# One place in each round for the score products, the value products and the transposes of two attentions, in a two-block network kernel

## The chip, the cores and the metric

The kernel runs on one core of one Trainium2 chip, in one launch. The metric is the device time of that launch in microseconds (us). TensorE (PE in the rows) does the matrix products and the transposes, and PEld is its weight load; ScalarE is ACT, VectorE is DVE, GpSimd is POOL, and SyncE (SP) issues most of the transfers.

## What is computed

A sequence of 512 tokens of width 1024 goes through two blocks of a network, all in fp32. The first block is a Mamba-2 mixer and then a layer of stick-breaking attention (16 heads of 64). The second is a gated linear recurrence beside a band attention (8 heads of 64), then a feed-forward network and a gated side input. The change touches the two attentions alone:

```python
# stick-breaking attention, for each block of 128 queries (lo..hi) and each head
z = jnp.einsum('bthd,bshd->bhts', q[:, lo:hi], k[:, :hi]) * scale
log_keep = jnp.where(mask, jax.nn.log_sigmoid(-z), 0.0)
after = lax.cumsum(log_keep, axis=3, reverse=True) - log_keep
a = jnp.exp(jnp.where(mask, jax.nn.log_sigmoid(z) + after, -jnp.inf))
outs.append(jnp.einsum('bhts,bshd->bthd', a, v[:, :hi]))
...
# band attention, second block
scores = jnp.einsum('bnqhd,bnkhd->bnhqk', qc, kb) * (B_HD ** -0.5)
probs = jax.nn.softmax(scores + bias, axis=-1)
o = jnp.einsum('bnhqk,bnkhd->bnqhd', probs, vb)
```

## The kernel before

Each large product of activations with a weight matrix is cut into output blocks of 128 features by 512 tokens. Both factors are split into a high and a low part, so each 128-row slice of the inner dimension takes three TensorE instructions, L658 (high by high), L659 and L660: a *step* of the text below. The activations' parts lie in HH and HL (SH and SL, WH and WL for some products), the weights' in whi and wlo. ScalarE makes whi from the loaded chunk (raw) with one instruction, L1985, and VectorE makes wlo (L1257).

Beside this dense stream run the attentions. Their work is cut into *units* a. A unit is a pair of heads and one block of 128 queries: 32 units in the stick-breaking attention, 16 in the band attention. The number of keys of a unit is 512, 384, 256, 128 for a mod 4 = 0, 1, 2, 3 in the first, and 128, 256, 384, 512 in the second, so that a tile of both heads has up to 1024 columns. A unit goes through these stages (the lines of the first attention first, of the band attention in brackets):

- TensorE: scores QK into PSUM tile zz, L985 (L1120), two products with 64 rows of weights
- first attention: ScalarE reads zz twice, sigmoid of -z and of z (L2319, L2320); VectorE scans (L1604) and multiplies (L1610). Band: VectorE reads zz with scale and bias (L1816), takes the maximum (L1818), ScalarE takes the exponential (L2475), VectorE divides (L1828, L1829)
- TensorE: transposes the weights into PSUM tile tt, L961 (L1095), 128x128 each
- ScalarE: copies tt to SBUF, L2325 (L2482)
- TensorE: values AV, L973 (L1108), products with 64 columns of weights, into bank 7; after each fourth unit ScalarE copies bank 7 out (L2330, L2490)

There is one zz and one tt. QK of unit a waits until zz is free of unit a-1 (semaphore s_bk, which L2320 raises; in the band s_bs, which L1816 raises), and the transposes of a wait until tt is free of a-1 (s_at; s_bt2).

Work of different units overlaps by *rounds* r. Each engine has a generator, `attention()` or `band()`, that yields three times in each round, and a generator with its share of the dense work. `weave` walks the two side by side in the ratio of their weights (111 to 120 in the first attention, 60 to 87 in the band), and so fixes the order of instructions on the engine: each engine runs strictly in that order. On TensorE the three places of round r hold the transposes of unit r-2, the values of r-3 and the scores of r+1. On ScalarE they hold the sigmoids of unit r, the copy of tt of unit r-2, and the copy of bank 7; between them `weave` puts what the dense work needs from ScalarE: the copy of a query block out of its bank (L2283), a tanh of a gate (L2302), SH from OZ (L2310) and the weights' whi (L1985).

Of the kernel before, what the change touches and what calls it, by code (L numbers as in the profile page):

```python
# [14 lines left out]
S = 512  # L15
# [183 lines left out]
def program(nc, wstream, astream, tstream, crow, vec, con, masks, xT, pT, rbx, out, scratch, pscr):  # L199
# [26 lines left out]
    zz, tt = (ctx.enter_context(nc.psum_tensor(n, [128, 2, S], F32)) for n in ("zz", "tt"))  # L226
# [33 lines left out]
    KT = sbt("KT", [128, NB, S], F32, ph)  # L260
    VT = sbt("VT", [128, 4, D], F32, ph)
    QT = sbt("QT", [128, NB, S], F32, ph)
# [18 lines left out]
    QB = sbt("QB", [128, 4, S], F32, phb)  # L281
    KB = sbt("KB", [128, 4, S], F32, phb)
# [20 lines left out]
    PS = [sbt(f"PS{i}", [128, 2, S], F32, ph3) for i in range(2)] + [TT3[:, 1:3, :]]  # L303
# [20 lines left out]
    ident, ones, bones = ccol("ident"), ccol("ones"), ccol("bones")  # L324
# [31 lines left out]
    s_kt, s_vt, s_qt, s_sz = (sem(n) for n in ("s_kt", "s_vt", "s_qt", "s_sz"))  # L356
    s_szt, s_qk, s_tr, s_av = (sem(n) for n in ("s_szt", "s_qk", "s_tr", "s_av"))
    s_bk, s_ls, s_at, s_o, s_go = (sem(n) for n in ("s_bk", "s_ls", "s_at", "s_o", "s_go"))
# [6 lines left out]
    s_off, s_ho, s_hoc, s_osq, s_osum, s_or, s_on, s_oah, s_oal = (  # L365
        sem(n) for n in ("s_off", "s_ho", "s_hoc", "s_osq", "s_osum", "s_or", "s_on", "s_oah", "s_oal"))
    s_qb, s_nsq, s_nsum, s_nr, s_qn, s_vb = (sem(n) for n in ("s_qb", "s_nsq", "s_nsum", "s_nr", "s_qn", "s_vb"))
    s_ga, s_wa, s_gb, s_wb, s_bw = (sem(n) for n in ("s_ga", "s_wa", "s_gb", "s_wb", "s_bw"))
    s_bq, s_bs, s_bm, s_be, s_bp, s_btr, s_bt2, s_bv, s_bo, s_obh, s_obl = (
        sem(n) for n in ("s_bq", "s_bs", "s_bm", "s_be", "s_bp", "s_btr", "s_bt2", "s_bv", "s_bo", "s_obh", "s_obl"))  # L370
# [74 lines left out]
    rows_of = lambda a: 3 - a % 4  # L445
    width = lambda a: 128 * (rows_of(a) + 1)
    att = lambda a, hi: W[:, 2 * (a % 4):2 * (a % 4) + 2, 0:hi]
    keeps = flat(W[:, 8:14, :])[:, 0:4 * (S + 1)].rearrange("p (a s) -> p a s", a=4)
    keep = lambda a, c0, c1: keeps[:, 2 * (a % 2):2 * (a % 2) + 2, c0:c1]
    live = lambda *units: [a for a in units if 0 <= a < 32]  # L450

    some = lambda a: [a] if 0 <= a < 16 else []
# [175 lines left out]
    def _(e):  # L628
        w = Once(e)
# [203 lines left out]
        for n, src in ((0, dd), (1, ac)):  # L833
            for c in range(4):
                o = 128 * n + 32 * c
                x = e.transpose(bank[:, o:o + 32], src[:, 128 * c:128 * c + 128], ident[0:32, 0:32])
# [4 lines left out]
                 start=True, stop=True).then_inc(s_sel, 1)  # L841
# [36 lines left out]
        for n in range(8):  # L878
            if n == 4:
                sum_of("out", aux[0])  # L880
            o, c = aux[1 + n % 4][:, :], slice(128 * n, 128 * n + 128)
# [3 lines left out]
            for k in range(2):  # L885
# [3 lines left out]
                x = e.matmul(o, wl[:, k, c], PH[:, k, :], start=False, stop=(k == 1))  # L889
# [61 lines left out]

        def attention():
            for r in range(-1, 36):
                for a in live(r - 2):
                    w.wait_ge(s_ls, a + 1)
                    w.wait_ge(s_at, a)
                    w.wait_ge(s_vt, 8)
                    for j in range(2):
                        for b in range(rows_of(a) + 1):
                            c = slice(128 * b, 128 * b + 128)  # L960
                            x = e.transpose(tt[:, j, c], att(a, S)[:, j, c], ident)  # L961
                    x.then_inc(s_tr, 1)
                yield
                for a in live(r - 3):
                    n, tb = a // 4, rows_of(a)
                    w.wait_ge(s_at, a + 1)
                    w.wait_ge(s_vt, 8)
                    if a % 4 == 0:
                        w.wait_ge(s_o, n)
                    for b in range(tb + 1):  # L970
                        for j in range(2):
                            h = 2 * n + j
                            x = e.matmul(aux[4][64 * j:64 * j + 64, 128 * tb:128 * tb + 128], VT[:, b, 64 * h:64 * h + 64],  # L973
                                         att(a, S)[:, j, 128 * b:128 * b + 128], start=(b == 0), stop=(b == tb))
                    x.then_inc(s_av, 1)
                yield
                for a in live(r + 1):
                    n, hi = a // 4, width(a)
                    w.wait_ge(s_qt, n + 1)
                    w.wait_ge(s_kt, n + 1)  # L980
                    w.wait_ge(s_vt, 6)
                    w.wait_ge(s_bk, a)
                    for j in range(2):
                        o = 64 * j
                        x = e.matmul(zz[:, j, 0:hi], QT[o:o + 64, n, hi - 128:hi], KT[o:o + 64, n, 0:hi],  # L985
                                     start=True, stop=True)
                    x.then_inc(s_qk, 1)
                yield

        proj = sb_proj()  # L990
# [1 line left out]
        next(proj)  # L992
        so_first = both("so", 0, "so")
        weave((attention(), 111), (chain(proj, take(so_first, 6)), 120))
        run(so_first)
        for n in range(2, 8):
# [12 lines left out]
        for t in range(4):  # L1009
            x = e.matmul(aux[4][:, t:t + 1], R[:, 128 * t:128 * t + 128], ident[:, 0:1], start=True, stop=True)  # L1010
# [75 lines left out]

        def band():
            for r in range(-1, 19):
                for a in some(r - 2):
                    w.wait_ge(s_bp, a + 1)  # L1090
                    w.wait_ge(s_bt2, a)
                    for j in range(2):
                        for b in range(a % 4 + 1):
                            c = slice(128 * b, 128 * b + 128)
                            x = e.transpose(tt[:, j, c], PS[a % 3][:, j, c], ident)  # L1095
                    x.then_inc(s_btr, 1)
                yield
                for a in some(r - 3):
                    n, tb = divmod(a, 4)
                    w.wait_ge(s_bt2, a + 1)  # L1100
                    w.wait_ge(s_vb, 4)
                    if tb == 0:
                        w.wait_ge(s_bo, n)
                        w.wait_ge(s_rc, 1)
                    for b in range(tb + 1):
                        for j in range(2):
                            h = 2 * n + j
                            x = e.matmul(aux[4][64 * j:64 * j + 64, 128 * tb:128 * tb + 128], VB[:, b, 64 * h:64 * h + 64],  # L1108
                                         PT[:, j, 128 * b:128 * b + 128], start=(b == 0), stop=(b == tb))
                    x.then_inc(s_bv, 1)  # L1110
                yield
                for a in some(r + 1):
                    n, tb = divmod(a, 4)
                    hi = 128 * (tb + 1)
                    w.wait_ge(s_qn, 8)
                    w.wait_ge(s_or, 4)
                    w.wait_ge(s_bs, a)
                    for j in range(2):
                        o = 64 * j
                        x = e.matmul(zz[:, j, 0:hi], QB[o:o + 64, n, 128 * tb:hi], KB[o:o + 64, n, 0:hi],  # L1120
                                     start=True, stop=True)
                    x.then_inc(s_bq, 1)
                yield

        def gates_a():
# [17 lines left out]
        dense_a = chain(gates_a(), branch_a())  # L1143
        run(take(dense_a, 5))
        weave((band(), 60), (dense_a, 87))
        for i2 in range(2):
            for n in range(4 * i2, 4 * i2 + 4):
# [1581 lines left out]
```

## Time and profile before

| | |
|---|---|
| time, median of 3 runs | 1557.64 us (1557.12 to 1559.62) |
| profiled execution, first to last instruction | 1557.7 us |
| TensorE busy | 1542.0 us, 99% |
| VectorE busy | 950.1 us, 61% |
| ScalarE busy | 678.2 us, 44% |
| mean granted clock of TensorE | 0.998 of full |
| first attention | about 523 to 669 us of the span |
| band attention | about 938 to 1035 us |

The profiled execution is one run of the same program. Its span agrees with the median of the runs to 0.1 us, and no other time of its own is listed. Starts in the trace's rows are in us from the start of the span. A matrix product's row gives its start and a modelled duration, and the durations of products in a row overlap, so that TensorE's pace is read from start to start.

### The profile page before, as it was taken

The page shows a single profiled execution, that of the slowest core. Times are in us where ns is not written, and L with a number is a line of the kernel's source. Part 1 is how long each engine was busy: PE and PEld are TensorE (multiplying, and loading weights), DVE is VectorE, ACT ScalarE, POOL GpSimd, SP SyncE. Part 2 cuts the span into 40 slices and gives each one's busy share as a digit, 9 for nine tenths or more (in the row PEclk, how much of TensorE's full clock was granted, in tenths as well). Part 3 has the DMA queues.
Part 4 walks back from the last instruction along what each step waited for, and adds up shares of the span by engine and source line. Part 5 has one row for each costly group of instructions (what it writes and reads, how often), then busy time and mean ns, then how long its engine had stood idle before and what let it go on. Part 6 is the DMA issues. An engine that isn't in the chain of part 4 may idle for free. (4 is left out here: it accounts for less than half of the span.)

```text
span 1557.7 us, 19286 instructions
## 1 busy us (share of the span) xinstructions
PE 1542.0 (99%) x7818; PEld 1220.9 (78%) x7818; DVE 950.1 (61%) x1211; ACT 678.2 (44%) x958; POOL 97.5 (6%) x66
## 2 busy tenths in 40 slices
PE   8999999999999999999999999999999999999998
PEld 4788887878788666678898886678888888888887
DVE  4769798996884666755468446754554434432445
ACT  4555676754432655654222455533342222322232
POOL 0000001011300000013000000000120000000110
PEclk9999999999999999999999999999999999999999
DMA  9245344433792111123211123222223222222233
GB/s 390 85 162 177 126 130 139 149 100 133 264 365 97 69 55 33 49 81 102 92 55 55 55 82 95 68 82 85 105 81 108 85 105 96 94 101 101 76 113 122
DMA packets 47383, 177.72 MB, mean 114 GB/s; under 512 B 3616, under 2 KB 20512, under 8 KB 31680
## 3 DMA queue, kind: packets, MB, share of 16 engines
q1 hardware_dynamic: 30368, 167.44, 30.2%
q10 hardware_dynamic: 16928, 9.06, 2.2%
q8 instruction: 62, 1.02, 0.3%
q14 instruction: 25, 0.20, 0.0%
HBM read 172.23 MB, written 4.26 MB: 113 GB/s over the span
## 5 line engine op out<-in xcount | busy, mean ns | idle before, releaser
L658 PE MATMUL bank<-HH,whi 128*128 128x512 f32 x1352 | 556.3, 411 | 0.5 <-issue 0.4
L660 PE MATMUL bank<-HH,wlo 128*128 128x512 f32 x1352 | 528.9, 391 | 0.0
L659 PE MATMUL bank<-HL,whi 128*128 128x512 f32 x1352 | 528.1, 391 | 0.0
L1257 DVE TENSOR_TENSOR wlo<-raw,whi 128x2048 fp32r<-128x2048 f32 (+2 forms) x122 | 267.2, 2190 | 105.7 <-ACT whi L1985 105.3
L658 PEld LDWEIGHTS bank<-HH,whi 128*128 128x128 f32 x1352 | 254.3, 188 | 81.0 <-issue 33.5
L660 PEld LDWEIGHTS bank<-HH,wlo 128*128 128x128 f32 x1352 | 254.2, 188 | 55.1
L659 PEld LDWEIGHTS bank<-HL,whi 128*128 128x128 f32 x1352 | 254.9, 189 | 47.9 <-issue 3.8
L1985 ACT ACTIVATE whi<-raw 128x2048 fp32r<-128x2048 f32 (+2 forms) x118 | 222.4, 1885 | 127.5 <-PE bank L660 108.2
L2587 POOL TENSOR_TENSOR SR<-SR,tmp 128x512 f32<-128x512 f32 x35 | 62.1, 1773 | 596.1 <-ACT tmp L2005 595.1
L1604 DVE TENSOR_TENSOR_SCAN W<-W,cc 128x511 f32<-128x511 f32 (+3 forms) x64 | 49.0, 808 | 34.6 <-ACT W L2320 34.5
L660 PE MATMUL bank<-FH,wlo 128*128 128x512 f32 x176 | 68.5, 389 | 0.0
L659 PE MATMUL bank<-FL,whi 128*128 128x512 f32 x176 | 68.5, 389 | 0.0
L658 PE MATMUL bank<-FH,whi 128*128 128x512 f32 x176 | 68.5, 389 | 0.0
L1916 DVE TENSOR_TENSOR pst<-bank,SR 128x512 f32<-128x512 f32 x22 | 15.1, 692 | 71.9 <-PE bank L660 71.9
L1928 DVE SCALAR_TENSOR_TENSOR tmp<-tmp,bank 128x512 f32<-128x512 f32 x22 | 15.1, 688 | 64.9 <-PE bank L660 64.9
L2556 ACT ACTIVATE FH<-tmp 128x512 fp32r<-128x512 f32 x22 | 13.9, 633 | 85.9 <-DVE tmp L1928 85.9
L2552 ACT ACTIVATE tmp<-pst 128x512 f32<-128x512 f32 x22 | 13.9, 633 | 82.4 <-DVE pst L1916 82.4
L2005 ACT ACTIVATE tmp<-X 128x512 f32<-128x512 f32 x35 | 21.6, 626 | 61.5 <-DVE X L1476 44.8
L2587 POOL TENSOR_TENSOR SR<-SR 128x512 f32<-128x512 f32 x12 | 19.9, 1662 | 340.7 <-ACT SR L2005 340.7
L2147 ACT ACTIVATE E<-AC,atk 128x128 f32<-128x128 f32 x128 | 39.1, 392 | 4.8 <-DMA AC<-scratch 4.8
L2319 ACT ACTIVATE W<-zz 128x1024 f32<-128x1024 f32 (+3 forms) x32 | 22.6, 708 | 41.1 <-PE zz L985 37.3
L658 PE MATMUL bank<-WH,whi 128*128 128x512 f32 x96 | 38.9, 405 | 0.0
(328 smaller groups left out, 2228.2 us busy)
## 6 DMA issues: line engine op xcount, KB each, us to landing
raw<-wstream SPq DMA_DIRECT2D x113, 1024.0 KB, 4.9
aslot<-tstream SPq DMA_DIRECT2D x24, 512.0 KB, 3.7
A<-astream SPq DMA_DIRECT2D x8, 1024.0 KB, 20.6
AC<-scratch ACTq DMA_DIRECT2D x16, 512.0 KB, 5.4
QT<-tstream SPq DMA_DIRECT2D x12, 512.0 KB, 6.5
OZ<-tstream SPq DMA_DIRECT2D x12, 512.0 KB, 7.7
raw<-wstream SPq DMA_DIRECT2D x4, 768.0 KB, 4.3
X<-xT SPq DMA_DIRECT2D x1, 2048.0 KB, 8.4
```

What stands on the lines that cost most here:

```text
L658: e.matmul(o, wh[:, k, c], hi[:, kb0 + k, :], start=first and k == 0, stop=False)
L659: e.matmul(o, wh[:, k, c], lo[:, kb0 + k, :], start=False, stop=False)
L660: x = e.matmul(o, wl[:, k, c], hi[:, kb0 + k, :], start=False, stop=last and k == kb - 1)
L1257: x = e.tensor_tensor(wlo[:, i % 2, c], raw[:, i % 2, c], whi[:, i % 2, c].bitcast(F32), ALU.subtract)
L1604: x = e.tensor_tensor_scan(k, k, diag[:, last], 0.0, ALU.mult, ALU.add)
L1916: e.tensor_tensor(pstage[n % 3][:, :], bank_of("fg", n)[:, :], R, ALU.mult).then_inc(s_fgr, 1)
L1928: e.scalar_tensor_tensor(q, q, 0.5, bank_of("fu", n)[:, :], ALU.mult, ALU.mult).then_inc(s_fu, 1)
L1985: e.activation(whi[:, i % 2, 0:n], raw[:, i % 2, 0:n], ACT.Copy).then_inc(s_hi, 1)
L2005: e.activation(dst, src, ACT.Square, scale=scale).then_inc(s_sq, 1)
L2147: x = e.activation(E[(u + 1) % 2][:, h, :], AC[:, h, :], ACT.Relu, scale=-1.0, bias=atk[:, cv_, 8 * gv + h:8 * gv + h + 1])
L2319: e.activation(keep(a, S - hi, S), zz[:, :, 0:hi], ACT.Sigmoid, scale=-1.0)
L2587: e.tensor_tensor(acc, acc, tile, ALU.add).then_inc(s_sqa, 1)
```

## The change

The three parts of a round on TensorE move to its third place, in the order scores of r+1, values of r-3, transposes of r-2. The first two places become empty. It is done in both attentions, and on no other engine does the order of instructions change.

```diff
         def attention():
             for r in range(-1, 36):
-                for a in live(r - 2):
-                    w.wait_ge(s_ls, a + 1)
-                    w.wait_ge(s_at, a)
-                    w.wait_ge(s_vt, 8)
+                yield
+                yield
+                for a in live(r + 1):
+                    n, hi = a // 4, width(a)
...
+                    w.wait_ge(s_bk, a)
                     for j in range(2):
...
+                        x = e.matmul(zz[:, j, 0:hi], QT[o:o + 64, n, hi - 128:hi], KT[o:o + 64, n, 0:hi],
+                                     start=True, stop=True)
+                    x.then_inc(s_qk, 1)
                 for a in live(r - 3):
                     n, tb = a // 4, rows_of(a)
                     w.wait_ge(s_at, a + 1)
...
                     x.then_inc(s_av, 1)
-                yield
-                for a in live(r + 1):
...
+                for a in live(r - 2):
+                    w.wait_ge(s_ls, a + 1)
+                    w.wait_ge(s_at, a)
+                    w.wait_ge(s_vt, 8)
                     for j in range(2):
...
+                            x = e.transpose(tt[:, j, c], att(a, S)[:, j, c], ident)
+                    x.then_inc(s_tr, 1)
                 yield
```

The change in `band()` is the same, with its own tiles and semaphores. In the changed file QK, AV and the transposes of the first attention stand at L964, L976 and L986, those of the band at L1099, L1112 and L1121.

TensorE in round 3 of the first attention, before: values of unit 0 (L973), scores of unit 4 (L985), transposes of unit 2 (L961), which belong to round 4, with a dense step between each.

```order
L973 MATMUL bank<-W,VT 64x128 x8
L658 MATMUL bank<-HH,whi 128x512
L659 MATMUL bank<-HL,whi 128x512
L660 MATMUL bank<-HH,wlo 128x512
L985 MATMUL zz<-KT,QT 128x512 x2
L658 MATMUL bank<-HH,whi 128x512
L659 MATMUL bank<-HL,whi 128x512
L660 MATMUL bank<-HH,wlo 128x512
L961 MATMUL tt<-cc,W 128x128 x4
```

The same place in the changed kernel: scores of unit 4 (L964), values of unit 0 (L976) and transposes of unit 1 (L986) of round 3.

```order
L658 MATMUL bank<-HH,whi 128x512
L659 MATMUL bank<-HL,whi 128x512
L660 MATMUL bank<-HH,wlo 128x512
L964 MATMUL zz<-KT,QT 128x512 x2
L976 MATMUL bank<-W,VT 64x128 x8
L986 MATMUL tt<-cc,W 128x128 x6
L658 MATMUL bank<-HH,whi 128x512
L659 MATMUL bank<-HL,whi 128x512
L660 MATMUL bank<-HH,wlo 128x512
```

The three parts now touch. From one such group to the next there are only dense steps: three of them, or four before the group that starts with the scores of unit 4, 8, 12, 16, 20, 25 or 29 (in the band four or five).

ScalarE around the same place, the same before and after, with the semaphores that each instruction waits for: the copy of tt of unit 1 (L2325, first row), the copy of a query block, the weights' whi, and the two sigmoids of unit 4.

```order
L2325 ACTIVATE W<-tt 128x2x384 [waits s_tr]
L2283 ACTIVATE QT<-bank 128x512 [waits s_blk]
L1985 ACTIVATE whi<-raw 128x2048 [waits l_raw1]
L2319 ACTIVATE W<-zz 128x2x512 [waits s_av,s_ls,s_qk]
L2320 ACTIVATE W<-zz 128x1024
L2325 ACTIVATE W<-tt 128x2x256 [waits s_tr]
```

Nothing moved here. The transposes that release the first row (s_tr) are now issued on TensorE behind the scores that release the fourth (s_qk); before, they were issued two places ahead of them.

## Rows read from the trace of the kernel before

**Rows 1.** The page: the span, and TensorE's busy time, share and instructions.

```profile
span 1557.7 us, 19286 instructions
PE 1542.0 (99%) x7818; PEld 1220.9 (78%) x7818; DVE 950.1 (61%) x1211; ACT 678.2 (44%) x958; POOL 97.5 (6%) x66
```

**Rows 2.** TensorE's timeline in the first attention: start, us, line, tile, count.

```profile
566.06 0.39 PE L660 MATMUL bank<-HH,wlo 128*128 128x512 f32 x1
566.38 0.70 PE L985 MATMUL zz<-KT,QT 64*128 64x256 f32 x4
567.01 0.50 PE L658 MATMUL bank<-HH,whi 128*128 128x512 f32 x1
567.35 0.39 PE L659 MATMUL bank<-HL,whi 128*128 128x512 f32 x1
567.58 0.39 PE L660 MATMUL bank<-HH,wlo 128*128 128x512 f32 x1
567.81 1.03 PE L961 MATMUL tt<-cc,W 128*128 128x128 f32 x8
568.60 0.48 PE L658 MATMUL bank<-HH,whi 128*128 128x512 f32 x1
...
569.15 0.40 PE L660 MATMUL bank<-HH,wlo 128*128 128x512 f32 x1
569.48 0.44 PE L973 MATMUL bank<-W,VT 128*64 128x128 f32 x4
569.85 0.50 PE L658 MATMUL bank<-HH,whi 128*128 128x512 f32 x1
```

**Rows 3.** TensorE's waits (us in total, times, longest), and one transpose that waited.

```profile
PE zz L718 <- DMA A<-astream: 3.2, 2, 2.3
...
PE tt L1095 <- DVE tmp L1829: 0.4, 1, 0.4
...
657.62 0.44 PE L961 MATMUL tt<-cc,W 128*128 128x128 f32 x2 [0.71 <-DVE W L1610]
```

**Rows 4.** ScalarE's timeline at three places of the first attention.

```profile
539.01 0.60 ACT L2283 ACTIVATE QT<-bank 128x512 f32<-128x512 f32 x1 [2.52 <-PE bank L660]
539.50 1.90 ACT L1985 ACTIVATE whi<-raw 128x2048 fp32r<-128x2048 f32 x1
541.31 1.02 ACT L2319 ACTIVATE W<-zz 128x1024 f32<-128x1024 f32 x1
542.21 1.03 ACT L2320 ACTIVATE W<-zz 128x1024 f32<-128x1024 f32 x1
543.11 0.61 ACT L2325 ACTIVATE W<-tt 128x512 f32<-128x512 f32 x1
...
568.88 1.02 ACT L2325 ACTIVATE W<-tt 128x1024 f32<-128x1024 f32 x1 [0.66 <-PE tt L961]
...
571.28 0.39 ACT L2319 ACTIVATE W<-zz 128x256 f32<-128x256 f32 x1 [0.71 <-PE zz L985]
...
628.53 0.81 ACT L2325 ACTIVATE W<-tt 128x768 f32<-128x768 f32 x1 [0.88 <-PE tt L961]
...
631.15 0.60 ACT L2302 ACTIVATE tmp<-bank 128x512 f32<-128x512 f32 x1 [1.32 <-PE bank L660]
631.65 1.14 ACT L2310 ACTIVATE SH<-OZ 128x512 fp32r<-128x512 f32 x2
```

**Rows 5.** VectorE's timeline in the band attention: the reads of zz of units 7 and 8.

```profile
973.77 1.22 DVE L1816 SCALAR_TENSOR_TENSOR PS<-zz,BW 128x1024 f32<-128x1024 f32 x1 [3.26 <-PE zz L1120]
...
980.90 0.42 DVE L1816 SCALAR_TENSOR_TENSOR tmp<-zz,BW 128x256 f32<-128x256 f32 x1
```

**Rows 6.** Windows: busy us of each engine, TensorE's granted clock, DMA share, GB/s.

```profile
24.00:29.00 5.00, 2.65 (x23) 1.42 (x22) 2.76 (x6) 3.34 (x4) 0.00 (x0) 0.98 1.01 418
29.00:36.00 7.00, 6.99 (x30) 4.31 (x30) 2.57 (x3) 0.37 (x2) 0.00 (x0) 0.52 1.01 418
523.00:669.00 146.00, 145.14 (x888) 93.95 (x888) 98.86 (x119) 84.59 (x124) 0.00 (x0) 1.00 0.15 50
```

More of the change, by code:

```diff
@@ L953, in attention @@
             for r in range(-1, 36):
-                for a in live(r - 2):
-                    w.wait_ge(s_ls, a + 1)
-                    w.wait_ge(s_at, a)
-                    w.wait_ge(s_vt, 8)
-                    for j in range(2):
[L959 to L962, printed above, removed]
-                yield
+                yield
+                yield
+                for a in live(r + 1):
+                    n, hi = a // 4, width(a)
+                    w.wait_ge(s_qt, n + 1)
+                    w.wait_ge(s_kt, n + 1)
+                    w.wait_ge(s_vt, 6)
+                    w.wait_ge(s_bk, a)
+                    for j in range(2):
+                        o = 64 * j
+                        x = e.matmul(zz[:, j, 0:hi], QT[o:o + 64, n, hi - 128:hi], KT[o:o + 64, n, 0:hi],
+                                     start=True, stop=True)
+                    x.then_inc(s_qk, 1)
                 for a in live(r - 3):
@@ L975, in attention @@
                     x.then_inc(s_av, 1)
-                yield
-                for a in live(r + 1):
[L978 to L982, printed above, removed]
+                for a in live(r - 2):
+                    w.wait_ge(s_ls, a + 1)
+                    w.wait_ge(s_at, a)
+                    w.wait_ge(s_vt, 8)
                     for j in range(2):
[L984 to L987, printed above, removed]
+                        for b in range(rows_of(a) + 1):
+                            c = slice(128 * b, 128 * b + 128)
+                            x = e.transpose(tt[:, j, c], att(a, S)[:, j, c], ident)
+                    x.then_inc(s_tr, 1)
                 yield
@@ L1088, in band @@
             for r in range(-1, 19):
-                for a in some(r - 2):
-                    w.wait_ge(s_bp, a + 1)
-                    w.wait_ge(s_bt2, a)
-                    for j in range(2):
[L1093 to L1097, printed above, removed]
+                yield
+                yield
+                for a in some(r + 1):
+                    n, tb = divmod(a, 4)
+                    hi = 128 * (tb + 1)
+                    w.wait_ge(s_qn, 8)
+                    w.wait_ge(s_or, 4)
+                    w.wait_ge(s_bs, a)
+                    for j in range(2):
+                        o = 64 * j
+                        x = e.matmul(zz[:, j, 0:hi], QB[o:o + 64, n, 128 * tb:hi], KB[o:o + 64, n, 0:hi],
+                                     start=True, stop=True)
+                    x.then_inc(s_bq, 1)
                 for a in some(r - 3):
@@ L1110, in band @@
                     x.then_inc(s_bv, 1)
[L1111 to L1117, printed above, removed]
+                for a in some(r - 2):
+                    w.wait_ge(s_bp, a + 1)
+                    w.wait_ge(s_bt2, a)
                     for j in range(2):
[L1119 to L1122, printed above, removed]
+                        for b in range(a % 4 + 1):
+                            c = slice(128 * b, 128 * b + 128)
+                            x = e.transpose(tt[:, j, c], PS[a % 3][:, j, c], ident)
+                    x.then_inc(s_btr, 1)
                 yield
```

## The prediction

> **What bounds the kernel now.** I read the page first. TensorE is busy for 1542.0 of 1557.7 us [rows 1], so whatever lengthens or shortens its queue lengthens or shortens the kernel. In the first attention it is busy for 145.1 of 146 us, at the full clock, with ScalarE at 85 us and VectorE at 99 [rows 6]. The change leaves every product in place, so two things can move the time: what it costs TensorE to pass from one kind of product to another, and waits. The timeline of TensorE shows the first. Inside the dense stream one product follows the last by 0.23 us (567.35 to 567.58), a step of three by 0.69. Around the attention's products the pace breaks [rows 2]:
>
> - into the scores 566.06 to 566.38, 0.32 instead of 0.23: 0.09 lost; behind them 567.01 to 567.35, 0.34: 0.11 lost
> - into the values 569.15 to 569.48, 0.33: 0.10 lost; behind them I take the same 0.11 as behind the scores
> - into the transposes 0.23, nothing lost; eight of them and the next product's start take 0.79, and 568.60 to 569.15 is 0.55 for two intervals, 0.09 above the pace, which the early start at 568.60 (0.24 before the transposes' modelled end) gives back.
>
> The scores use 64 rows of the array, the values 64 columns, the transposes and the dense products all of it. The loss goes with the change of shape. (The Trainium skill, TensorEngine Tiling (Array Packing), section Key Properties, says that changing the tiling mode drains TensorE. The rows agree, at about 0.2 us for a change and back.)
>
> **What the change saves.** Before, a round has four changes of shape: into and out of the scores, into and out of the values. After it has three: dense to scores, scores to values, values to transposes; from transposes to dense is free as now. A joint of scores and values drops the 0.11 behind the scores and the 0.10 ahead of the values: 0.21. A joint of values and transposes drops the 0.11 behind the values, and pays for a reload that nothing covers. Two transposes that had waited took 0.44 [rows 3], where two at the pace of [rows 2] take 1.03 - 6 x 0.11 = 0.37; I take 0.06, so the joint saves 0.05.
>
> - First attention: scores and values both stand in rounds 3 to 30, 28 x 0.21 = 5.9. Transposes have something ahead of them in rounds 2 to 33, 32 x 0.05 = 1.6. Together 7.5.
> - Band: rounds 3 to 14, 12 x 0.21 = 2.5, and 16 x 0.05 = 0.8. Together 3.3.
>
> No joint of two such shapes stands in the trace of before, so I bound it. Below: a joint saves nothing, 0. Above: everything but the entry into the scores is saved, some 0.4 us a round, 40 rounds, 16 us. I take 10.8, by the rows for the same changes next to dense products.
>
> The transposes come two places later, so VectorE has more time ahead of them. Its late results at L961 (0.71 us) and L1095 (0.4) are then covered [rows 3]: 1.1 saved.
>
> **What the change adds: a loop through ScalarE.** ScalarE's order does not change. In it the copy of tt of unit a-3 stands ahead of the sigmoids of unit a. The scores of unit a+1 need zz free, so they wait for the second sigmoid of a. Before, the transposes of a-3 were issued two places ahead of the scores of a; ScalarE had made their copy by then, or made it behind the sigmoids of the unit before, and waited for the scores (0.71 us at 571.28 [rows 4]). After, those transposes are the last part of the group that begins with the scores of a. ScalarE can only start its copy when the whole group is done, and TensorE has three or four dense steps until it wants zz again. What does not fit stops TensorE, and the dense steps behind it in its queue too.
>
> What TensorE covers, from the transposes' end E: the next product starts at E - 0.24, the first step takes 0.55 and each further one 0.69, and the scores come 0.32 behind the last L660. With three steps that is -0.24 + 0.55 + 1.39 + 0.32 = 2.02 us, with four 2.71.
>
> What ScalarE needs [rows 4]: it starts 0.04 after E (567.81 + 1.03 [rows 2], to 568.88). Then every instruction costs the distance to the next, which is its time less about 0.11 (541.31 to 542.21 is 0.90 for 1.02); the last sigmoid counts in full, and 0.05 for the signal. By width, 1024 columns take 1.02, 768 0.81, 512 0.60, 256 0.39.
>
> - a mod 4 = 0: copy of 768, sigmoids of 1024: 0.04 + 0.70 + 0.91 + 1.02 + 0.05 = 2.72
> - 1: copy 512, sigmoids 768: 0.04 + 0.49 + 0.70 + 0.81 + 0.05 = 2.09
> - 2: copy 256, sigmoids 512: 1.46
> - 3: copy 1024, copy of bank 7 (512), sigmoids 256: 2.16
>
> Plain rounds: units 8, 12, 16 and 20 wait 0.70 each, 28 nothing (four steps), 5, 13, 17, 21 and 25 wait 0.07, 23 and 27 (three steps) 0.14. Sum 3.4.
>
> Six rounds carry dense work of ScalarE between the copy and the sigmoids: the query copy costs 0.49 (539.01 to 539.50), whi 1.81 (539.50 to 541.31), a tanh 0.50, two SH 1.04.
>
> - a = 4: query copy and whi, 2.72 + 2.30 - 2.02 = 3.0
> - a = 9: the same, 2.09 + 2.30 - 2.02 = 2.4
> - a = 14: the same, 1.46 + 2.30 - 2.02 = 1.7
> - a = 19: two tanh and whi, 2.16 + 1.00 + 1.81 - 2.71 = 2.3
> - a = 24: two tanh, two SH, whi, 2.72 + 1.00 + 1.04 + 1.81 - 2.71 = 3.9
> - a = 29: whi, 2.09 + 1.81 - 2.02 = 1.9
>
> Sum 15.2; with the plain rounds 18.6 us. These whi copies cost nothing today, because ScalarE idles for 61 of the 146 us and the loop is not closed. The waits are not given back later: the next round starts from the next group's end.
>
> In the band the loop goes through VectorE: its read of zz of unit a now also waits for the transposes of a-3, because of the PS buffer. One read takes 1.22 us at most, against four or five steps (2.7 us or more). The worst place is unit 8, which starts 7.13 us after unit 7 with VectorE full between [rows 5], against some 7.6 us of TensorE until the scores that need it. I put 0.1. The copies of tt and the exponentials have a round to spare.
>
> Sum at the full clock, against the profiled execution's 1557.7 (the median of the runs is the same to 0.1): 1557.7 - 7.5 - 3.3 - 1.1 + 18.6 + 0.1 = 1564.5.
>
> **The clock.** TensorE waited 2.3 us for a transfer (L718 [rows 3]); it was busy for 2.65 of the 5 us around that, and the 7 us that followed show a granted clock of 0.52, the 1.2 GHz level [rows 6]. That costs 7 x 0.48 = 3.4 us of work. Today nothing in the attentions waits as long. After the change four waits are 2.3 us or more. The longest, at a = 24, is far above the one that was followed by a fall, and I count one fall: 1564.5 + 3.4 = 1567.9. No fall and a fall at each of the six are the bounds, 1564.5 and 1584.9. (The Trainium skill, TensorE: Matmul & The Clock Gate, section Why this matters for your kernels, says that idle gaps between bursts of products send TensorE back to the lower clock. The trace agrees, with the one gap above.)
>
> **The rivals.**
>
> - *The loop is closed, and the clock falls at most of the long waits.* For it, the fall after 2.3 us. Against it, that some of the waits are shorter, and that a single gap is all the trace shows. Three to six falls: 1574.7 to 1584.9. 0.14.
> - *The joints save nothing*, each change of shape costing its full price whatever comes next. 1564.5 + 10.8 = 1575.3, with a fall 1578.7. Against it, that the 0.11 behind the scores belongs to dense weight loads that are no longer there. 0.07.
> - *Faster: whi is not on the loop.* If the six dense pieces of ScalarE were done while TensorE works through the group, ahead of the copy of tt, their waits would shrink to those of plain rounds (about 2): 1557.7 - 11.9 + 3.4 + 2 = 1551, faster. It decides below 8.8 us of waits in sum. For it, that ScalarE idles there. Against it, the order, in which L2325 stands ahead of L2283 and L1985. 0.12.
> - *No change within the measurement*: the waits come out at two thirds, the joints near their upper bound. 0.11.
> - *The forecast*: waits of about 18.6, joints about 10.8, none to two falls, 1561 to 1573. 0.56.
>
> **How the numbers follow.** A measurement tells 0.2% (3 us) from no change. Slower holds the forecast and the first two rivals, 0.77; within 0.2% 0.11; faster 0.12. The likeliest case has one fall: 1567.9. The range runs from 1557, which leaves out the faster rival, to 1579, which leaves out four and more falls.
>
> **What would show it.** Right: L2325 waits for L986 and is followed without idle time by L2319; TensorE shows six waits of 1.7 to 3.9 us ahead of L964 for ScalarE's L2320, and no wait in the band; L976 follows L964 with no dense product between and 0.2 us less is lost; the page shows a lower clock in one slice about 630 us. Wrong: scores that wait for VectorE's L1610 (through the sigmoids), a joint that costs more than the two it replaces, or a clock at 1.0 throughout, which takes 3.4 off.

## The result, and the profile after

The changed kernel takes 1571.13 us (median of 4 runs, 1570.09 to 1572.5) against 1557.38 us for the kernel before (4 runs, 1557.11 to 1559.62) on the same chip: a ratio of 1.0087, interval 1.0075 to 1.0099. It is slower by 13.75 us. The ratios here and below are taken over all runs, so they can lie up to 0.001 from the quotient of the medians. The profiled execution took 1570.73 us, and its span is 1568.9: in every run of this study the time is 1.8 to 2.2 us more than the span. One execution of one version, a sixth of e6_tail_apart below, took 5393.53 us for a reason that nothing on record shows, and is left out.

The page of the changed kernel, the lines that answer to [rows 1]:

```profile
span 1568.9 us, 19251 instructions
PE 1536.0 (98%) x7818; PEld 1227.5 (78%) x7818; DVE 949.8 (61%) x1211; ACT 676.7 (43%) x958; POOL 97.5 (6%) x66
```

TensorE is busy for 6 us less than before, and the span is 11.2 us longer. So the busy time went down, although the clock fell in places (below), and TensorE stands idle for 17 us more. The view of TensorE's waits (us in total, times, longest) says where; they answer to [rows 3]:

```profile
PE zz L964 <- ACT W L2320: 17.3, 10, 3.8
PE zz L718 <- DMA A<-astream: 2.3, 1, 2.3
PE bank L658 <- issue: 2.0, 2, 1.6
...
PE bank L658 <- DVE OZ L1585: 0.8, 1, 0.8
...
PE zz L1099 <- DVE PS L1816: 0.3, 1, 0.3
```

The first row is new and as large as the idle time that was added: the scores wait for the second sigmoid of the unit before. The rows of L961 and L1095 are gone. The rows of L1585 and of 1.6 us for "issue" are new too, and no step of the prediction named them.

**The loop at its first long wait.** TensorE's timeline of the changed kernel at the scores of unit 5:

```profile
542.47 1.29 PE L964 MATMUL zz<-KT,QT 64*128 64x384 f32 x4 [2.91 <-ACT W L2320]
543.68 1.55 PE L976 MATMUL bank<-W,VT 128*64 128x128 f32 x12
545.16 1.12 PE L986 MATMUL tt<-cc,W 128*128 128x128 f32 x4
```

and ScalarE's ahead of it:

```profile
537.49 0.81 ACT L2325 ACTIVATE W<-tt 128x768 f32<-128x768 f32 x1 [4.08 <-PE tt L986]
538.20 0.59 ACT L2283 ACTIVATE QT<-bank 128x512 f32<-128x512 f32 x1
538.68 1.91 ACT L1985 ACTIVATE whi<-raw 128x2048 fp32r<-128x2048 f32 x1
540.48 1.03 ACT L2319 ACTIVATE W<-zz 128x1024 f32<-128x1024 f32 x1
541.38 1.04 ACT L2320 ACTIVATE W<-zz 128x1024 f32<-128x1024 f32 x1
```

ScalarE idles for 4.08 us until the group's transposes (L986) are through. Then five instructions follow each other without a gap, and the scores start 0.05 us behind the last of them, at 542.42 + 0.05. Before, in [rows 4], the same query copy and whi stand ahead of the sigmoids, and TensorE did not wait for them.

**The joints.** A group of the changed kernel at the full clock:

```profile
588.49 0.40 PE L660 MATMUL bank<-HH,wlo 128*128 128x512 f32 x1
588.87 0.70 PE L964 MATMUL zz<-KT,QT 64*128 64x256 f32 x4
589.51 0.66 PE L976 MATMUL bank<-W,VT 128*64 128x128 f32 x8
590.10 0.44 PE L986 MATMUL tt<-cc,W 128*128 128x128 f32 x2
590.29 0.48 PE L658 MATMUL bank<-HH,whi 128*128 128x512 f32 x1
590.60 0.40 PE L659 MATMUL bank<-HL,whi 128*128 128x512 f32 x1
```

From the scores to the values it is 0.64 us (588.87 to 589.51), as long as from the same scores to a dense product in [rows 2] (566.38 to 567.01, 0.63). So the values' entry costs nothing of its own, and the slow second product behind the scores (0.34 instead of 0.23 in [rows 2]) is gone: 0.10 + 0.11 = 0.21 saved. From the first of eight transposes to the next dense product it is 0.85 us behind values (575.00 to 575.85, not shown) and 0.79 behind a dense product [rows 2], 0.06 more, so that the other joint saves 0.11 - 0.06 = 0.05 to 0.06. A whole group without a wait, from the last dense product ahead of it to the second behind it, takes 0.25 to 0.29 us less than its three parts took apart, in both attentions.

**The clock.** Windows of the changed kernel, columns as in [rows 6]; the last but two figures are the granted clock, DMA share and GB/s:

```profile
541.90:546.00 4.10, 3.53 (x21) 2.29 (x21) 3.52 (x3) 0.52 (x1) 0.00 (x0) 0.62 0.00 0
569.00:573.50 4.50, 4.50 (x21) 3.42 (x22) 3.90 (x5) 1.36 (x3) 0.00 (x0) 0.63 0.00 0
573.50:642.90 69.40, 63.49 (x411) 44.12 (x410) 38.99 (x48) 34.51 (x54) 0.00 (x0) 1.00 0.14 46
642.90:652.00 9.10, 5.33 (x25) 3.57 (x25) 6.99 (x10) 4.83 (x6) 0.00 (x0) 0.63 0.00 0
```

Three times the granted clock fell to the 1.2 GHz level, at the waits of units 5, 10 and 25 (3.0, 2.4 and 3.8 us). By the clock's share of each window it was low for 3.1, 3.3 and 6.7 us, where the first window ends inside the fall; windows of 0.2 us give 3.4, 3.4 and 6.8 us. The first two falls begin 0.4 and 1.2 us after the scores have started, the third at about 645.2, inside the wait, which ends at 646.73. Before, the attention ran at 1.00 [rows 6]. The waits at units 20 (2.2 us), 30 (1.9) and 15 (1.7) were followed by none. The other three runs of the changed kernel have a mean clock of 0.994 to 0.996 too, where the runs of the kernel before beside the experiments have 0.997 to 1.0, which speaks for falls of about the same length in each.

**Behind the attention.** Three places of the changed kernel's TensorE, the second of the waits being that for "issue":

```profile
688.96 0.47 PE L658 MATMUL bank<-SH,whi 128*128 128x512 f32 x1 [0.81 <-DVE OZ L1585]
...
695.57 0.44 PE L976 MATMUL bank<-W,VT 128*64 128x128 f32 x4
...
703.24 0.47 PE L658 MATMUL bank<-SH,whi 128*128 128x512 f32 x1 [1.56 <-issue]
```

with ScalarE's timeline

```profile
686.79 0.60 ACT L2325 ACTIVATE W<-tt 128x512 f32<-128x512 f32 x1 [3.35 <-PE tt L986]
687.28 0.59 ACT L2302 ACTIVATE tmp<-bank 128x512 f32<-128x512 f32 x1
...
696.78 0.63 ACT L2310 ACTIVATE SH<-OZ 128x512 fp32r<-128x512 f32 x1 [4.32 <-DVE OZ L1570]
697.43 1.28 ACT L1996 ACT_TABLE_LOAD   x1
698.72 1.92 ACT L1985 ACTIVATE whi<-raw 128x2048 fp32r<-128x2048 f32 x1
```

and VectorE's.

```profile
687.91 0.69 DVE L1585 SCALAR_TENSOR_TENSOR OZ<-tmp,bank 128x512 f32<-128x512 f32 x1 [5.20 <-ACT tmp L2302]
...
696.05 0.69 DVE L1570 SCALAR_TENSOR_TENSOR OZ<-bank,OZ 128x512 f32<-128x512 f32 x1 [4.75 <-PE bank L976]
...
700.84 2.29 DVE L1257 TENSOR_TENSOR wlo<-raw,whi 128x2048 fp32r<-128x2048 f32 x1 [2.63 <-ACT whi L1985]
```

The first wait comes from one of the last transposes: ScalarE's copy of them (L2325) stands ahead of the tanh (L2302), VectorE's L1585 needs the tanh, and TensorE needs the OZ of L1585. The second comes from the last values. From them (695.57) a chain runs over OZ, SH, a table load, whi and wlo (ready at 703.13) to the product at 703.24: 7.67 us. Before, the same chain ran from 679.87 to 687.54, 7.67 us as well, but 10 dense steps stood in it; now the last values come two steps later in the stream and 8 are left. So TensorE waits longer at its end: 1.72 us beyond the pace, where it was 0.36 before, 1.4 us more.

**The balance.** I set the first products of some stages in both traces against each other. The stretch ahead of the first scores is 2.06 us shorter after; there the clock fell for 3.4 us instead of 7 [rows 6], and in the runs below that stretch varies between 519.7 and 523.0 us whatever the kernel. The first attention (first scores to last values) is 17.76 us longer, the band (first scores to the same dense product behind it in both) 4.50 us shorter, everything else equal within 0.04 us. -2.06 + 17.76 - 4.50 = 11.2, the difference of the spans. Without the chance of the first stretch it is 13.26, near the 13.75 of the medians.

The 17.76 us are made up like this. The waits ahead of L964, each taken from start to start less the plain 0.32, are 18.5 (units 5, 10, 15, 20, 25, 30: 3.0, 2.4, 1.7, 2.2, 3.8, 1.9; the others 3.5). Two more dense steps stand in the stretch, 1.4, which the stretch behind it no longer has (there the wait for wlo takes their place). L1585 gives 1.0. The joints give back 28 x 0.21 + 32 x 0.06 = 7.8, the transposes that waited for VectorE 1.2. That makes 11.9, and 5.9 are left for the clock.

### The profile page after: what moved, and what is told of

Its sections match the earlier page's. It is cut to its first block and busy times, and to the rows that moved or that the text cites. A ratio compares the mean times of both kernels' runs of the same rounds, so it can differ in the third digit from the quotient of the medians.

```text
span 1568.9 us, 19251 instructions
## 1 busy us (share of the span) xinstructions
PE 1536.0 (98%) x7818; PEld 1227.5 (78%) x7818; DVE 949.8 (61%) x1211; ACT 676.7 (43%) x958; POOL 97.5 (6%) x66
## 5 line engine op out<-in xcount | busy, mean ns | idle before, releaser
L658 PE MATMUL bank<-HH,whi 128*128 128x512 f32 x1352 | 548.3, 406 | 0.4 <-issue 0.4
L1985 ACT ACTIVATE whi<-raw 128x2048 fp32r<-128x2048 f32 (+2 forms) x118 | 222.4, 1885 | 125.2 <-PE bank L660 106.0
L2325 ACT ACTIVATE W<-tt 128x1024 f32<-128x1024 f32 (+3 forms) x32 | 22.6, 706 | 82.1 <-PE tt L986 82.1
L964 PE MATMUL zz<-KT,QT 64*128 64x512 f32 (+3 forms) x128 | 27.0, 500 | 17.5 <-ACT W L2320 17.3
```

What stands on the lines that cost most here:

```text
L658: e.matmul(o, wh[:, k, c], hi[:, kb0 + k, :], start=first and k == 0, stop=False)
L1985: e.activation(whi[:, i % 2, 0:n], raw[:, i % 2, 0:n], ACT.Copy).then_inc(s_hi, 1)
L2325: e.activation(att(a, hi), tt[:, :, 0:hi], ACT.Copy).then_inc(s_at, 1)
```

## The experiments

The theory: the loop through ScalarE adds the waits, each fall of the clock behind a wait adds to them, and the joints save what [rows 2] show. Its rivals: the joints cost or save nothing, so that the waits would have to be smaller; or the loss comes from the group as such, whatever its order.

**1. The change in one attention alone.** The diff of the section above, in `attention()` alone (e1_first_only) or in `band()` alone (e2_band_only).

> The change in the first attention alone; the band attention stays as before. Theory (a loop through ScalarE, falls of the clock behind its long waits, and two waits behind the attention): the stretch from the first scores to the last values is 17.8 us longer than before, as in the changed kernel, so 1557.4 + 17.8 = 1575.2 us, slower than the whole change, with L964 waiting some 18.5 us for L2320. Rival (part of the loss comes from the band): 1571 us or less.

> The change in the band attention alone. Theory (joints save 12 x 0.20 + 16 x 0.05 = 3.2 us, and the late transposes 1.0 us, no loop of note): 1557.4 - 4.4 = 1553.0 us, faster. Rival (a change of shape costs the same in a joint as next to dense products): 1557.4 - 1.0 = 1556.4 us.

Measured: 1576.19 us for the first (ratio 1.0115, 1.0102 to 1.0129) and 1553.23 for the second (0.9968, 0.9956 to 0.9979), the kernel before at 1558.01 beside both. +18.2 and -4.8 add up to 13.4: the two parts are independent, and the band is a gain. In the band the waits for VectorE (L1095 [rows 3] and L1120) fall from 1.3 to 0.6 us; most of the rest are the joints. Windows of e1_first_only around its own falls of the clock:

```profile
538.00:548.00 10.00, 7.09 (x39) 4.62 (x39) 5.31 (x5) 5.20 (x6) 0.00 (x0) 0.83 0.00 0
614.00:622.00 8.00, 5.83 (x34) 4.15 (x33) 4.73 (x9) 3.43 (x6) 0.00 (x0) 0.79 0.01 2
642.00:652.00 10.00, 6.54 (x35) 4.05 (x37) 7.37 (x11) 5.41 (x6) 0.00 (x0) 0.83 0.00 0
668.00:676.00 8.00, 6.20 (x28) 4.16 (x26) 7.93 (x11) 4.17 (x6) 0.00 (x0) 0.79 0.00 0
```

Its six long waits are those of the changed kernel within 0.1 us, but the clock fell behind units 5, 20, 25 and 30, and not behind 10. So which of the waits brings a fall differs from one execution to the next. In the two executions together all waits of 1.9 us and more did so at least once.

**2. Scores and values together, transposes left in the first place** (e3_scores_values; first attention only, against before).

```diff
                     x.then_inc(s_tr, 1)
                 yield
-                for a in live(r - 3):
...
-                    x.then_inc(s_av, 1)
                 yield
                 for a in live(r + 1):
...
                     x.then_inc(s_qk, 1)
+                for a in live(r - 3):
...
+                    x.then_inc(s_av, 1)
                 yield
```

> First attention only: scores and values together in the third place, transposes left in the first place. Theory: 28 joints of scores and values save 28 x 0.20 = 5.6 us, the loop through ScalarE stays open because the copy of tt is released two places ahead of the scores, so no wait of L2320 above a tenth and no fall of the clock. The last values come one place later than before, which may cost up to 1.7 us behind the attention, as in the changed kernel. 1557.4 - 5.6 + 1.7 = 1553.5 us (1551.8 without that wait). Rival (any group of attention products at the third place closes the loop): slower than before, above 1565 us.

Measured: 1554.03 us (0.9974, 0.9964 to 0.9983), no wait for L2320 at all, and the clock at 1.00 in the attention. The first attention is 3.94 us shorter although two more dense steps (1.4) and 0.2 of wait stand in it: 28 joints saved 5.5, 0.20 each. So the joint of scores and values is a gain, and the waits need the transposes behind the scores.

**3. The dense pieces of ScalarE ahead of the copy of tt** (e4_dense_first; the changed kernel, with ScalarE's two copies moved directly ahead of the next sigmoids).

```diff
         def attention():
             for r in range(-1, 36):
+                for a in live(r - 3):
...
+                    w.wait_ge(s_tr, a + 1)
+                    e.activation(att(a, hi), tt[:, :, 0:hi], ACT.Copy).then_inc(s_at, 1)
...
                 for a in live(r):
...
                 yield
-                for a in live(r - 2):
...
-                    e.activation(att(a, hi), tt[:, :, 0:hi], ACT.Copy).then_inc(s_at, 1)
                 yield
```

> The changed kernel, with one edit on ScalarE: in the first attention the copy of tt and the copy of bank 7 stand directly ahead of the next unit's sigmoids, so that the weights' whi, the query copies, the tanh and SH come ahead of them and not between. Theory: the six long waits shrink to those of plain rounds, from 15.0 to about 2 us, the clock no longer falls (5.7 us), 1571.1 - 13.0 - 5.7 = 1552.4 us; L2320 is still waited for by some 5.5 us in all. Rival (the long waits are set by something else that ends at the same time, as VectorE's L1610): six long waits remain, 1571 us within 3 us.

Measured: 1553.31 us (0.9968, 0.9956 to 0.998). TensorE's order is that of the changed kernel, word for word; an order on ScalarE alone gives back 18 us. ScalarE's timeline at the same unit, where whi now stands ahead of the copy and in ScalarE's idle time:

```profile
534.67 1.90 ACT L1985 ACTIVATE whi<-raw 128x2048 fp32r<-128x2048 f32 x1
537.07 0.81 ACT L2317 ACTIVATE W<-tt 128x768 f32<-128x768 f32 x1 [0.49 <-PE tt L986]
537.78 1.02 ACT L2327 ACTIVATE W<-zz 128x1024 f32<-128x1024 f32 x1
538.68 1.03 ACT L2328 ACTIVATE W<-zz 128x1024 f32<-128x1024 f32 x1
```

Its waits:

```profile
PE zz L964 <- ACT W L2328: 5.5, 7, 1.7
```

What is left is the 0.7 us of the plain rounds, and one of 1.73 us at 655.59, behind which the clock fell for 3.4 us, where the expectation had no fall. So a fall can follow a wait of that length.

**4. The clock's share, by products in the waits** (e5_filled, e9_filled_less). The changed kernel, with extra fp32 products of 512 columns into tt ahead of the scores that follow a long wait; nothing reads their values. The first fills more than the waits, the second less.

```diff
+        FILL = {5: 6, 10: 5, 15: 3, 20: 4, 25: 8, 30: 4}
...
+                    if a in FILL:
+                        w.wait_ge(s_at, a - 3)
+                        for _ in range(FILL[a]):
+                            e.matmul(tt[:, 0, :], ones, X[:, 0, :], start=True, stop=True)
                     w.wait_ge(s_bk, a)
```

> The changed kernel, where TensorE computes extra products into the free tile tt, whose values nobody reads, just ahead of the six scores that wait long: 6, 5, 3, 4, 8 and 4 products of 512 columns (0.43 us each) ahead of the scores of units 5, 10, 15, 20, 25 and 30, so that they end before the sigmoid that is waited for. The waits are the same, but TensorE is busy in them. Theory (part of the loss is the clock that falls behind idle waits, about 5.7 us): the granted clock stays at 1.0 in the attention, the stretch from the first scores to the last values is 12 us longer than before instead of 17.8, 1571.1 - 5.7 = 1565.4 us. Rival (the clock's fall costs nothing, because ScalarE sets the pace there): 1571 us.

Measured: 1576.37 us (1.0117, 1.0104 to 1.0131). I had taken a product at half its price: each stands in the trace as two instructions, and the six at unit 5 take 4.82 us (539.68 to 544.50), 0.8 each, so that they outlast the wait that they should fill.

```profile
539.68 4.88 PE L966 MATMUL tt<-X,cc 128*128 128x512 f32 x11
544.50 0.92 PE L970 MATMUL zz<-KT,QT 64*128 64x384 f32 x4
```

The granted clock stayed at 1.00 in the whole attention, but the run does not price the falls. So the fill was cut to fit:

```diff
-        FILL = {5: 6, 10: 5, 15: 3, 20: 4, 25: 8, 30: 4}
+        FILL = {5: 3, 10: 2, 15: 1, 20: 2, 25: 4, 30: 2}
```

> As the filled version, with half the extra products, since its trace shows that one product of 512 columns in fp32 takes TensorE 0.86 us (two passes of 0.43) and not 0.43, so that the extra work outlasted the waits by some 10 us. Now 3, 2, 1, 2, 4 and 2 products, 2.6, 1.7, 0.9, 1.7, 3.4 and 1.7 us of work in waits of 3.0, 2.4, 1.7, 2.2, 3.8 and 1.9 us. Theory (about 5.7 us of the loss is the clock that falls behind idle waits): the granted clock stays at 1.0 in the attention, first scores to last values 12 us longer than before instead of 17.8, 1571.1 - 5.7 = 1565.4 us. Rival (the fall costs nothing): 17.8 us longer, 1571 us.

Measured: 1565.08 us (1.0042, 1.003 to 1.0055), and the whole first attention at the full clock:

```profile
530.00:684.00 154.00, 147.88 (x914) 100.66 (x914) 94.58 (x118) 79.86 (x121) 0.00 (x0) 1.00 0.14 49
```

(The expectation's 0.86 us for a product is 0.80 in the trace.) The waits are now mostly filled: 5.0 us are left idle, none longer than 0.8. The attention is 12.31 us longer than before, not 17.76: the falls of the clock cost 5.4 us in the changed kernel's profiled execution (5.7 by the spans; 6.0 by the medians, or 7.6 when each median is set against the kernel before that ran beside it, whose own runs lie in two groups 2 us apart). 12.31 also agrees with the 11.9 of the balance above.

**5. The last rounds apart** (e6_tail_apart; the changed kernel, but in rounds 32 and later transposes and values stand in their old places, the first and the second).

```diff
             for r in range(-1, 36):
+                if r >= 32:
+                    for a in live(r - 2):
...
                 yield
+                if r >= 32:
+                    for a in live(r - 3):
...
                 yield
...
+                if r < 32:
```

> The changed kernel, but in rounds 32 to 35 of the first attention the transposes and values go back to the first and second place. Theory (the two late dense steps behind the attention, 0.9 and 1.7 us, come from the last transposes and the last values being issued later, with ScalarE's tanh, SH and whi queued behind them): both waits go, the joints of these rounds (0.15 us) too: 2.4 us less, about 1568.7 us. The falls of the clock may differ by 3.4 us between two executions, so the waits in the trace decide more than the time. Rival (they come from ScalarE being late after unit 29): they stay, 1571 us.

Measured: 1568.98 us (1.0069, 1.0056 to 1.0082), 2.15 less than the changed kernel. Its waits from 660 us on:

```profile
PE zz L987 <- ACT W L2344: 1.8, 1, 1.8
PE bank L658 <- issue: 0.2, 1, 0.2
```

L1585 is gone and "issue" is back at 0.2, so both tail waits (1.0 and 1.36 us, together 2.3) come from the places to which the last transposes and values were moved. In its attention the clock fell four times, for 3.4 us each.

**6. Other orders of the group** (e7_scores_last: transposes, values, scores, and the band as changed; e8_joint_and_band: e3_scores_values with the last rounds apart, and the band as changed).

```diff
             for r in range(-1, 36):
+                yield
+                yield
                 for a in live(r - 2):
...
                     x.then_inc(s_tr, 1)
-                yield
                 for a in live(r - 3):
...
                     x.then_inc(s_av, 1)
-                yield
                 for a in live(r + 1):
```

(This is e7's first attention against the kernel before.)

> The changed kernel, with the order within a round of the first attention turned round: transposes, values, scores. All three still touch. Theory: ScalarE copies tt while TensorE does values and scores, only the sigmoids are left behind the group's end (2.0 us for the widest), and zz is wanted again only behind the next group's transposes and values, so no wait for L2320 of note and no fall of the clock; the joints save about as much as in the changed order. First scores to last values about 5 us shorter than before, 1558.0 - 5 - 4.5 = 1548.5 us. Rival (any grouping of the three closes the loop, whatever the order): above 1565 us.

> A version put together from what the runs showed: in the first attention transposes in the first place, scores and values together in the third, the values of the last rounds in the second as before; the band attention as in the changed kernel. Theory: 5.6 us from joints of scores and values, 4.5 us from the band, no wait behind the attention: 1558.0 - 10.1 = 1547.9 us. Rival (the two do not add, since dense work of the first attention comes late at its end): 1550 us or more.

Measured: 1547.41 us (0.9936, 0.9924 to 0.9948) and 1548.11 us (0.9937, 0.9925 to 0.9949). In e7 all three parts touch, as in the changed kernel, and only their order differs. The transposes open the group, ScalarE copies tt while TensorE works on the values and scores, and of 17.3 us of waits 0.3 are left. That refutes the rival that the group as such is the loss. The wait for wlo (1.6) stays, since the last values are still two steps late. In e8 the gains of e3 and of the band add up as expected.

**7. The best of both** (e10_scores_last_tail: e7 with the last rounds apart; e11_both_scores_last: e10 with transposes, values, scores in the band too).

> The order transposes, values, scores in one place for rounds up to 31 of the first attention, and the places of before in rounds 32 to 35; band attention as in the changed kernel. Theory: as the version with the scores last, less its wait of 1.6 us for the weights behind the attention and its change of shape there: first scores to last values 7.2 us shorter than before, 1547.5 - 1.7 = 1545.8 us. Rival (that wait comes from ScalarE's queue earlier on): 1547.5 us.

> As the one before, with the order transposes, values, scores in the band attention too. Theory: the joints of the band cost the same in either order, its loop through VectorE had no wait above 0.3 us, so at most 0.4 us less: 1545.5 us. Rival (the transposes, now first, wait for VectorE's late results again): up to 1 us more, 1546.8 us.

Measured: 1546.15 us (0.9922, 0.9909 to 0.9936) and 1546.43 us (0.993, 0.9917 to 0.9944). The first has the lowest median of the study, 12.8 us below the kernel before that ran beside it (1558.95; 12.2 by the ratio), and can't be told from e11. TensorE's timeline of one of its groups:

```profile
583.12 0.40 PE L660 MATMUL bank<-HH,wlo 128*128 128x512 f32 x1
583.36 1.04 PE L987 MATMUL tt<-cc,W 128*128 128x128 f32 x8
584.32 0.44 PE L998 MATMUL bank<-W,VT 128*64 128x128 f32 x4
584.69 0.49 PE L1009 MATMUL zz<-KT,QT 64*128 64x128 f32 x4
585.11 0.50 PE L658 MATMUL bank<-HH,whi 128*128 128x512 f32 x1
```

and ScalarE's beside it:

```profile
582.62 0.60 ACT L2343 ACTIVATE W<-zz 128x512 f32<-128x512 f32 x1
583.10 0.61 ACT L2344 ACTIVATE W<-zz 128x512 f32<-128x512 f32 x1
584.43 1.03 ACT L2349 ACTIVATE W<-tt 128x1024 f32<-128x1024 f32 x1 [0.72 <-PE tt L987]
585.35 0.59 ACT L2354 ACTIVATE QT<-bank 128x512 f32<-128x512 f32 x1
585.83 0.39 ACT L2343 ACTIVATE W<-zz 128x256 f32<-128x256 f32 x1
```

The copy of tt (L2349) starts at 584.43, ahead of the group's scores at 584.69; the sigmoids follow without a gap, and TensorE passes. The band loses 0.5 us by the same order (e11, 92.79 against 92.25 us from its first scores to its last values), which the medians can't tell from nothing: there VectorE reads the scores, and no loop was closed. Transposes wait for VectorE nowhere in it, so the expectation's rival is not what costs the 0.5; its groups take about 0.04 us more each than in the order of the change.

## Why the prediction was right, and where it was off

The forecast was slower, 1567.9 us, for a measured 1571.1. Against the profiled execution's 1557.7 it summed to +10.2; measured is +13.3 without the chance of the first stretch. The 1557.7 is a span, and that it equals the median time is luck: a time is some 2 us more than its span, and the profiled execution was slower than the median by as much, in its first stretch. By the prediction's own steps:

- **The loop through ScalarE** (18.6 us): measured 18.5. The six long waits were forecast as 3.0, 2.4, 1.7, 2.3, 3.9, 1.9 and came as 3.0, 2.4, 1.7, 2.2, 3.8, 1.9, at the places named; e4 and e7 show in two different ways what makes them: the place of the transposes behind the scores, and the dense pieces of ScalarE behind the copy. The rows of L2325, L2283, L1985 and L2319 above show whi behind the copy although its operands were there, since e4 starts the same whi at 534.67. (The Trainium skill, PSUM — Partial Sum Buffer, section Engine vs sequencer instructions, says that ScalarE's queue is strictly first in, first out. These rows agree.) The rival "whi is not on the loop" fails by the same rows; e4 is what it would have been. What was to be seen of it was seen: L2325 waits for L986, and no gap stands between it and L2319.
- **The joints** (7.5 and 3.3): 7.8 and 3.5. The rival that they save nothing is out by e3 and e2, and so is the upper bound of 16 us.
- **Late transposes** (1.1): 1.2 in the first attention. In the band 0.7 net: its late transposes (0.85, where I had read one of 0.4) went. A wait of 0.4 us for L1816 at unit 1 stood there before and stayed, and one of 0.22 came at unit 9, behind the read of unit 8 that I had named, where I had put 0.1 and written "no wait in the band". The two attentions together are 1.9 where 1.0 was summed.
- **The clock** (one fall, 3.4): this step was mis-sized. There were three falls, 13.6 us at half the clock, a part of it while TensorE waited anyway, and they cost 5.4 us by e9 and 5.9 by the balance. I had taken the one fall in the trace, 7 us long behind a wait of 2.3, for a mark that only the longest wait would pass. The falls seen here last 3.4 or 6.8 us and come behind waits from 1.7 us, but not behind each; what decides it stays open. Hence the rival "falls at most of the long waits" was right in the mechanism for three of six, but took each at 3.4 us of loss, where a fall of 3.4 us costs half of that. The sign that I had named, a lower clock in one slice of the page, did not come: its clock row shows 9 in all slices, since even 6.8 us at half the clock in a slice of 39 take off less than a tenth. Only the windows show the falls.
- **The tail** (not in the sum): 2.3 us. This is the term that I had left out without a reason. I followed the joints to the last round, but not what the last transposes and values release: behind them stand the tanh, SH, whi and wlo that the next stage waits for.

The terms that were off add up to 2.0 to 2.5 (clock), +2.3 (tail), -0.5 (joints), -0.9 (late transposes): 2.9 to 3.4 us, against the 3.1 that the sum lacked. So part of the closeness is luck: costs of 4.3 us and more were missed, and savings of 1.4 stood against them. The range, 1557 to 1579, holds the result. It does not do what I wrote of it: four falls at my own price give 1578.1, inside it, and only five and more are left out.

## What to carry to other kernels

When parts on a busy engine are moved together, look at which of them releases work of another engine that the *next* group needs, and put that part first: the same three parts cost 13.8 us in one order and gave 10.3 in the other (e7, with the band alike in both). Work of an in-order engine that was free because the engine idled lands on the path as soon as it stands between the late release and the awaited result; add up everything in that queue, not the one instruction that is waited for. And look at the last round by itself: what is free to come later in the steady state may open the next stage.

## What the runs showed of the hardware

- Between scores (64 rows) and values (64 columns) a change of shape costs 0.2 us less than through dense products. Directly from values to scores (e10) the next product's start comes 0.37 us behind the values (584.32 to 584.69), as it does before a dense product [rows 2] (569.48 to 569.85): no entry price for the scores. Transposes behind values take 0.06 us more for eight.
- TensorE's clock fell to 1.2 GHz for 3.4 or 6.8 us behind waits of 1.7 to 3.8 us in some executions and not in others of the same program, at different waits each time. (The Trainium skill, TensorE: Matmul & The Clock Gate, section Why this matters for your kernels, says that idle gaps between bursts bring the lower clock. The runs agree, for gaps down to 1.7 us, and in e9, with the gaps mostly filled, none came in the attention.)
- An fp32 product of 512 columns with 128 rows and columns of weights took 0.8 us, in two instructions (e5), where a dense product of the same size, on operands that ScalarE and VectorE write as fp32r, is followed by the next after 0.23.
